# GpSimd adds up the squares, TensorE multiplies two sums with ones, in seven norms of a three-layer decoder on one core

## The reference

```
def rms_norm(x, g, eps=RMS_EPS):
    xf = x.astype(jnp.float32)
    y = xf * lax.rsqrt(jnp.mean(xf * xf, axis=-1, keepdims=True) + eps)
    return (y * g.astype(jnp.float32)).astype(x.dtype)

x = x + memory_cross_attention(rms_norm(x, norm_mem[i]), mem, ...)
x = x + swiglu(rms_norm(x, norm_ffn[i]), ffn_w_gate[i], ffn_w_up[i], ffn_w_down[i])
```

## Time and profile before

| | |
|---|---|
| time, median of 3 runs | 1430.54 us (1429.88 to 1431.63) |
| time of the profiled execution | 1429.88 us |
| its span | 1428.1 us |
| TensorE matmuls, busy | 1326.5 us, 93% |
| VectorE busy | 919.7 us, 64% |
| ScalarE busy | 586.8 us, 41% |
| GpSimd busy | 61.7 us, 4% |
| chain that ended last, by engine | PE 72%, DVE 18%, issue 5%, ACT 2% |
| mean granted TensorE clock | 0.914 of full speed |

### The profile page before, as it was taken

One profiled execution on the slowest core, in us unless ns is written; L12 is line 12 of the kernel. 1 busy time (PEld: TensorE's weight loads), 2 busy tenths in 40 slices (PEclk: granted clock), 3 DMA queues, 4 the chain that ended last, 5 costly groups with the idle time before them and its releaser, 6 DMA issues.

```text
span 1428.1 us, 25070 instructions
## 1 busy us (share of the span) xinstructions
PE 1326.5 (93%) x9306; PEld 1218.2 (85%) x9306; DVE 919.7 (64%) x1654; ACT 586.8 (41%) x1003; POOL 61.7 (4%) x52
## 2 busy tenths in 40 slices
PE   5899989899999999989999999999799976999996
PEld 5888879799999999668899999989656666899996
DVE  5876347576665577645657666577853346999955
ACT  4644344454444522424344444533533323444441
POOL 0554100000000000000000000000000000000000
PEclk9999999999999999559999999999955568999998
DMA  6434344245555544102325555534410003355462
GB/s 243 145 120 147 118 155 170 79 158 178 187 191 180 181 174 150 58 1 95 142 89 177 176 183 191 209 136 165 155 53 1 1 4 116 118 176 172 162 213 73
DMA packets 29589, 194.19 MB, mean 136 GB/s; under 512 B 3152, under 2 KB 6352, under 8 KB 6352
## 3 DMA queue, kind: packets, MB, share of 16 engines
q1 hardware_dynamic: 29520, 193.22, 39.1%
HBM read 192.16 MB, written 1.05 MB: 135 GB/s over the span
## 4 chain that ended last, share of the span: by engine, by line
PE 72%; DVE 18%; issue 5%; ACT 2%; DVEq 1%; DMA 1%; ACTq 0%; SPq 0%
PE acc L405 17%; PE acc L407 16%; PE acc L406 16%; PE acc L421 8%; PE sc L588 6%; DVE wlo L978 4%; PE acc L609 3%; PE tp L600 2%; DVE wlo L975 2%; PE sc L591 1%; ACT whi L715 1%; DVE E L1173 1%; DVE nw L1027 1%; DVE nw L1026 1%; PE st L561 1%
## 5 line engine op out<-in xcount | busy, mean ns | idle before, releaser
L405 PE MATMUL acc<-Hhi,whi 128*128 128x256 f32 x1504 | 435.7, 290 | 39.3 <-DVE wlo L978 24.5
L406 PE MATMUL acc<-Hlo,whi 128*128 128x256 f32 x1504 | 427.8, 284 | 0.0
L407 PE MATMUL acc<-Hhi,wlo 128*128 128x256 f32 x1504 | 427.7, 284 | 0.0
L715 ACT ACTIVATE whi<-raw 128x1024 fp32r<-128x1024 f32 x164 | 173.4, 1057 | 476.5 <-PE acc L407 445.8
L405 PEld LDWEIGHTS acc<-Hhi,whi 128*128 128x128 f32 x1504 | 290.9, 193 | 47.1 <-issue 23.7
L406 PEld LDWEIGHTS acc<-Hlo,whi 128*128 128x128 f32 x1504 | 291.0, 194 | 2.1 <-issue 1.9
L407 PEld LDWEIGHTS acc<-Hhi,wlo 128*128 128x128 f32 x1504 | 290.8, 193 | 0.0
L975 DVE TENSOR_TENSOR wlo<-raw,whi 128x1024 fp32r<-128x1024 f32 x164 | 200.8, 1224 | 136.0 <-ACT whi L715 134.6
L405 PE MATMUL acc<-FH,whi 128*128 128x256 f32 x848 | 243.4, 287 | 20.9 <-DVE wlo L978 5.2
L407 PE MATMUL acc<-FH,wlo 128*128 128x256 f32 x848 | 242.9, 286 | 0.0
L978 DVE TENSOR_TENSOR wlo<-raw,whi 128x1024 fp32r<-128x1024 f32 x164 | 202.0, 1232 | 0.0
(11 more groups left out here) (213 smaller groups left out, 1702.5 us busy)
## 6 DMA issues: line engine op xcount, KB each, us to landing
raw<-weights SPq DMA_DIRECT2D x180, 1024.0 KB, 4.9
cst<-consts SPq DMA_DIRECT2D x1, 1126.0 KB, 12.3
X<-x_in SPq DMA_DIRECT2D x1, 1024.0 KB, 6.1
MEM<-mem_in SPq DMA_DIRECT2D x1, 1024.0 KB, 14.4
out<-X SPq DMA_DIRECT2D x4, 256.0 KB, 2.2
PT<-positions SPq DMA_DIRECT2D x1, 128.0 KB, 14.2
cst<-consts SPq DMA_DIRECT2D x1, 32.0 KB, 1.9
```

The costliest lines, as they stand in the source:

```text
L405: pe.matmul(dst, w, x, start=first, stop=False)
L406: pe.matmul(dst, w, xl, start=False, stop=False)
L407: return pe.matmul(dst, wl, x, start=False, stop=last)
L715: act.activation(whi[j][:, 0:HALF, :], raw[j][:, 0:HALF, :], ACT.Copy).then_inc(hi_out, 1)
```

## The change

In seven norms (`mem0`, `ffn0`, `attn1`, `mem1`, `ffn1`, `pre2`, `fpre2`) GpSimd adds each of the pairs 1 to 3 of squares onto pair 0, in place, as soon as ScalarE has written it. TensorE waits for GpSimd's new semaphore `squares_summed` in place of `s_sq` and multiplies two chunks with ones in place of eight; in `pre2` two and two in place of eight and eight. In all 48 matmuls go, and 24 additions of 128x512 elements come (three a norm, six in `pre2`).

```
+        squares_summed = sem("squares_summed")
+        SUMMED = ["mem0", "ffn0", "attn1", "mem1", "ffn1", "pre2", "fpre2"]
...
         @block.gpsimd
...
+            for name in SUMMED:
+                sources = [SQ, SQF] if name == "pre2" else [SQ]
+                for p in range(1, 4):
+                    pool.wait_ge(s_sq, sq.at(SQ_OF[name], p + 1))
+                    for q in sources:
+                        ins = pool.tensor_tensor(out=q[:, 0:2, :], in0=q[:, 0:2, :], in1=q[:, 2 * p:2 * p + 2, :], op=ALU.add)
+                        if p < 3 or q is not sources[-1]:
+                            pc.link(ins)
+                ins.then_inc(squares_summed, 1)
...
                     if norm_name:
-                        pe.wait_ge(s_sq, sq.at(SQ_OF[norm_name]))
+                        if norm_name in SUMMED:
+                            pe.wait_ge(squares_summed, SUMMED.index(norm_name) + 1)
+                        else:
+                            pe.wait_ge(s_sq, sq.at(SQ_OF[norm_name]))
+                        chunks = 2 if norm_name in SUMMED else DC
                         if norm_name == "pre2":
-                            norm_stats("final")
-                        norm_stats(norm_name, SQF if norm_name == "pre2" else SQ)
+                            norm_stats("final", chunks=chunks)
+                        norm_stats(norm_name, SQF if norm_name == "pre2" else SQ, chunks=chunks)
...
-            def norm_stats(name, src=SQ, ready=None):
+            def norm_stats(name, src=SQ, ready=None, chunks=DC):
...
-                for k in range(DC):
+                for k in range(chunks):
...
-                    mm = pe.matmul(st[:, 0:S], ones[:, :], src[:, k, :], start=k == 0, stop=k == DC - 1)
+                    mm = pe.matmul(st[:, 0:S], ones[:, :], src[:, k, :], start=k == 0, stop=k == chunks - 1)
```

## The result

| | before | after |
|---|---|---|
| median of 4 runs, us | 1430.21 (1429.55 to 1431.63) | 1440.26 (1438.78 to 1440.54) |
| profiled execution / span, us | 1429.88 / 1428.1 | 1438.78 / 1436.5 |
| TensorE busy, us; matmuls recorded | 1326.5; 9306 | 1317.7; 9210 |
| VectorE busy, us | 919.7 | 929.9 |
| mean granted TensorE clock | 0.914 | 0.905 |

After over before is 1.0063, 95% interval 1.0049 to 1.0077: 9 us slower (0.63% of 1430.2; the two medians are 10 apart). The forecast was 1439.0 in a range of 1430.5 to 1446. (The prediction took the 16 records of the earlier trace rows for eight weight loads and eight matmuls; the 0.43 us a matmul is the same either way.) Yet TensorE's busy time fell by 8.8 us only, not by 20.7: the other matmuls took longer.

A forecast was written before the change was run, and what follows sets the result against it. The prediction took VectorE's way from tile 0 to tile 2, not TensorE's 93% busy time, as the bound: removal 0, lock 5.3, clock 3.4, so 1429.88 + 5.3 + 3.4 = 1438.6, median 1439; range 1430.5 to 1446 us.

The forecast's parts named there:

- The removal is worth nothing: In the seven norms, 48 matmuls (20.7 us) go, but VectorE's way decides when tile 2 starts; value 0.
- the predicted signs: Norm's first instruction no earlier behind `lower`; TensorE waiting 1.7 to 3 us ahead of each third tile, before 0.4.
- TensorE's time comes back: Rival: TensorE's way decides, not VectorE's, in the changed norms; 20.7 us less, 1410, or part of it; chance 0.05.
- The sums come late but not too late: In `mem0` the last addition ends about 232.0, TensorE idles 1.1 us, sums by 233.0 before VectorE's 234.40; cost 0.
- The lock: GpSimd's additions hold VectorE off the shared port in `attn1`, `pre2` and `fpre2`; 5.3 us, bounds 0 and 30 us.
- `fpre2` 2.54: In `fpre2` two additions of 1.27 us push into VectorE's run of six `Hlo`, which TensorE awaits; cost 2.54 us.
- `pre2` 0.96: At pair 3 in `pre2`, two additions run until 944.70, so L975 starts then in place of 943.74; cost 0.96 us.
- pair 3 of `attn1` 0.51: In `attn1` GpSimd gets the port at 496.64; L975 of the next tile starts 499.05, not 498.54; cost 0.51 us.
- pair 1 of `attn1` 1.27: In `attn1` an addition pushes back L978, due at 463.77, for which TensorE already waits; cost 1.27 us.
- The clock: Behind longer gaps TensorE's clock falls, 1.7 us a slow stretch; two stretches taken, 3.4 us, bounds 0 and 10.2.
- one in `pre2`: One of the two slow clock stretches taken falls behind the gaps of `pre2`; 1.7 us lost per stretch.
- a stretch behind `fpre2` would be hidden: Behind a 2.9 us gap in `fpre2` a slow stretch is hidden, since TensorE soon waits for VectorE again.

The follow-up runs named there:

- e1: After without GpSimd's additions, sums of two chunks only, so the removal of the 48 matmuls alone; 1434.74 us against before's 1431.32, ratio 1.0028.
- e10: Before plus tile 0 copied out early, GpSimd adding pairs 1 and 2, four chunks multiplied in mem0, ffn0, mem1, ffn1; repeat run, 1418.54 us, ratio 0.9914 to before.
- e2: After with all 24 additions, but TensorE still multiplying eight chunks without waiting for them: the additions alone; 1434.77 us, ratio 1.0026 to before.
- e7: Before plus tile 0 copied out early, GpSimd adding pairs 1 and 2, four chunks multiplied in mem0, ffn0, mem1, ffn1; first run, 1420.04 us, ratio 0.9922 to before.
- e4: After with matmuls whose result nobody uses filling TensorE's gaps; 1435.18 us, ratio 1.0032 to before.
- e8: Before with GpSimd adding pairs 1 and 2 and TensorE multiplying four chunks in mem0, ffn0, mem1, ffn1, no early copy; 1434.9 us, ratio 1.0024 to before.
- e3: Before with the whole change in the norm fpre2 alone; 1434.21 us, ratio 1.0022 to before.
- e9: Before plus tile 0 copied out early, two chunks multiplied and no additions in mem0, ffn0, mem1, ffn1 (sums incomplete); 1419.54 us, ratio 0.9919 to before.

## Why the prediction was right, and where not

**The removal is worth nothing: right.** It rested on the norm's first instruction standing without idle time behind `lower` and on the small waits for the copies. e1 shows it with nothing beside it but the clock behind the longer gaps; the predicted signs (L1033 where it was, a wait of 1.7 to 3 us ahead of tile 2) are in after's rows at 1.64, 1.87, 1.91, 1.80 and 2.94 us. Theory "TensorE's time comes back" is refuted, and e10 shows the condition under which it would have been right: the accumulator's bank must not wait for the norm.

**The sums come late but not too late: right, to the decimal.** 232.0 and 1.1 us of idle TensorE were foreseen for `mem0`; 231.96 (230.05 + 1.91) and 1.04 came.

**The lock: the mechanism right, its sum 5.3 us against 3.2 in the trace and 3.7 in e2.** By term: `fpre2` 2.54, measured 2.0; `pre2` 0.96, measured 0.88; pair 3 of `attn1` 0.51, measured 0.3; pair 1 of `attn1` 1.27, measured 0. The last is a step that failed. "L978 would start at 463.77 and is pushed back by 1.27 us", said the prediction. After, against the earlier trace rows:

```profile
464.16 1.22 DVE L992 TENSOR_TENSOR wlo<-raw,whi 128x1024 fp32r<-128x1024 f32 x1
...
464.89 2.77 POOL L407 TENSOR_TENSOR SQ<-SQ 128x512 f32<-128x512 f32 x1 [160.91 <-ACT SQ L784]
465.29 1.22 DVE L995 TENSOR_TENSOR wlo<-raw,whi 128x1024 fp32r<-128x1024 f32 x1
...
466.43 2.31 DVE L992 TENSOR_TENSOR wlo<-raw,whi 128x1024 fp32r<-128x1024 f32 x1
466.57 0.39 PE L418 MATMUL acc<-FH,whi 128*128 128x256 f32 x1 [1.28 <-DVE wlo L995]
```

GpSimd's addition was issued at 464.89, ahead of L995, and yet L995 took the port at 465.29 and ran its usual 1.22 us. GpSimd waited through it (2.77 less 1.27 is 1.50 us) and then held up the next L992, for which nobody waits; TensorE's gap stays at 1.28. The same happened to pair 3 (`POOL` at 497.83, 2.68 us). The prediction took from the earlier trace rows that GpSimd "gets it when it has waited", and that was one case. Even at the place of the earlier trace rows, in the convolution, it does not always hold. There the second of two additions on `SQ` is issued 0.06 or 0.07 us behind the start of a `lower`, in every trace. In that of e7 GpSimd came next and held up the second `lower`:

```profile
44.94 4.80 POOL L392 TENSOR_TENSOR SQ<-SQ 128x1024 f32<-128x1024 f32 x2 [44.49 <-ACT SQ L893]
47.37 1.22 DVE L1002 TENSOR_TENSOR wlo<-raw,whi 128x1024 fp32r<-128x1024 f32 x1
48.51 2.32 DVE L1005 TENSOR_TENSOR wlo<-raw,whi 128x1024 fp32r<-128x1024 f32 x1
```

In that of e10, the same kernel, the second `lower` came next, and the two additions took 5.93 us in place of 4.80:

```profile
44.29 5.93 POOL L392 TENSOR_TENSOR SQ<-SQ 128x1024 f32<-128x1024 f32 x2 [43.84 <-ACT SQ L893]
46.71 1.22 DVE L1002 TENSOR_TENSOR wlo<-raw,whi 128x1024 fp32r<-128x1024 f32 x1
47.85 1.22 DVE L1005 TENSOR_TENSOR wlo<-raw,whi 128x1024 fp32r<-128x1024 f32 x1
```

The Trainium skill's "SBUF — State Buffer", section "Who interferes with whom", has the lock held by whoever comes first. That neither engine works while the other holds it, this trace bears out (2.31 and 2.11 us for a `lower` that meets an addition). For a request made while the port is taken, "first" would have meant GpSimd at 464.89; the row shows VectorE. The measurement decides: a waiting GpSimd has no claim on the next turn.

**The clock: 3.4 us foreseen, about 4.0 to 4.4 measured (e1; after less e4).** Five stretches behind gaps are in after's trace that before lacks, and one of before's is missing there. The forecast of one in `pre2` fits (948 to 958 and 962 to 968, part of it in TensorE's waits), and so does the one that a stretch behind `fpre2` would be hidden. Outside `pre2` the forecast counted one more that costs; in the four plain norms, whose gaps are the shortest, there were two: behind 1.91 us at 688.73 and 1.80 us at 761.23 the clock fell, behind 1.64 us at 240.52 and 1.87 us at 312.79 it did not.

So 5.3 + 3.4 = 8.7 was close to 9.0 with one term too large and one too small; that the total was better than its parts is luck.

## What to carry to other kernels

Time taken off the busiest engine is worth what the next wait behind it leaves: follow the gap that would grow, to the instruction that ends it, and ask what that one waits for. Where it is a buffer held for a late factor, free the buffer first (copy it out raw, scale it later); only then does removing work pay, here 11 us in four norms, in place of a loss of 9 in seven. And a helper on GpSimd is not free while VectorE streams from SBUF, nor is a gap on TensorE free, since the clock behind it may be halved.

## What the runs showed of the hardware that was not expected

Who gets the shared port next, when GpSimd asks for it during a VectorE instruction and VectorE has another that needs it, does not follow from how long ahead GpSimd asked, by the recorded starts. At the place of the earlier trace rows, asked for 1.07 us before VectorE's next instruction starts, GpSimd came next in six traces (before, e4 to e8) and VectorE in six (after, e1, e2, e3, e9, e10). At pair 1 and pair 3 of `attn1`, asked 0.40 and 0.34 us ahead (464.89, 497.83), VectorE came next in all three traces that have these additions (after, e2, e4). Behind an `Hlo` it was GpSimd, though it asked only 0.31 us ahead: the two that follow take 1.91 us, where the two ahead of them, undisturbed, take 0.88 (after, 481.42 and 480.62; the addition at 481.11). What does settle it is open.

Matmuls whose result is thrown away, 2 to 6 a gap, made after 4.4 us faster (1.0063 to 1.0032); behind the filled gaps the granted clock stayed at its upper level, 2.4 GHz.

A gap does not decide the clock alone: behind the same 2.08 us (272.74 before, 272.76 after) the granted clock was 1.00 in one trace and 0.72 in the other, and 0.72 in e3's, whose program is the same up to there as before's.
